# A three-block model on one core: x laid out twice, the first unit taken up as it arrives, weights split sooner, six output blocks sharing the first half

## The chip, the cores and the metric

The kernel runs on one core of one Trainium2 chip (trn2). The metric is the device time in microseconds (us). The engines are PE (TensorE: matmuls, with weight loads on its own queue PEld), DVE (VectorE), ACT (ScalarE), POOL (GpSimd) and SP (SyncE), which only issues DMAs here. They meet only through semaphores.

## What is computed

x is 512 tokens by 1024 features. Three layers follow one another: a gated linear recurrence (RG-LRU) with its MLP, a sparse attention layer with its MLP, and a second block of gated linear attention with a gated MLP. The change touches the first mixer alone:

```python
def rms_norm(x, g):
    y = xf * lax.rsqrt(jnp.mean(xf * xf, axis=-1, keepdims=True) + EPS)
    return y * g

def rglru_mixer(h, w_in, conv_w, conv_b, w_a, b_a, w_x, b_x, lam, w_out):
    gate, xr = jnp.split(h @ w_in, 2, axis=-1)          # 1024 -> 2 x 1024
    gate = jax.nn.gelu(gate)
    xc = conv_b + sum(xpad[:, k:k + S] * conv_w[k] for k in range(4))
    r = sigmoid(xc blockwise @ w_a + b_a); i = sigmoid(xc blockwise @ w_x + b_x)   # 4 blocks of 256
    log_a = -8 * r * softplus(-lam)
    a = exp(log_a); u = sqrt(-expm1(2 * log_a)) * (i * xc)
    hs = scan of h_t = a_t * h_{t-1} + u_t
    return (hs * gate) @ w_out
```

(The reference cut to this; `x = x + mix` and `x = x + mlp(rms_norm(x))` follow.)

## The kernel before, in words

**Layout.** Activations lie with features on the partitions: X, Ahi and Alo are eight blocks of 128 features by 512 tokens. Each product of float32 values is made of three matmuls in a 32-bit format with a shorter mantissa: hi times hi, lo times hi, hi times lo (`three`, L797 to L800). So every operand is split: ACT rounds it to the high part, DVE subtracts to get the low part.

**Units.** Weights come in units of 1024 by 256 (1 MB), numbered in the order in which they are used: 0 to 3 are xr (the recurrent half of w_in), 4 and 5 the two gate matrices (ga), 6 to 9 gate (the other half of w_in), 10 to 13 ro (w_out), then the MLP. A unit goes through `stage[u % 2]`, and there are two buffers each of `whi` and `wlo`. `hi(u)` on ACT (L1283) waits for the load and for the last product of unit u-2; `lo(u)` on DVE (L1791) waits for `hi(u)`; SP's `load(u)` (L552) waits for `lo(u-2)`; PE's `take_unit` waits for `lo(u)`. Unit 12 (ro 2) has hi and lo buffers of its own, inside Ahi and Alo.

**Blocks and banks.** A unit gives two blocks of 128 outputs by 512 tokens. Each of them takes one of six PSUM banks in a fixed ring order; `begin` waits until the bank's owner six places earlier has been read out. A full block is 24 matmuls of 512 columns; a block of ga is 6.

**Order of the work.** Every engine's order is written out by hand. PE: transposes of the identity, transposes of x, xr 0 and 1 in two halves of 256 tokens (L868), xr 2, the root (four matmuls that spread 1/rms over the partitions, L856), xr 3 to 7, ga (16 short blocks), gate 0 to 7, then ro: blocks 0 to 3 run over features 0 to 3 first and over 4 to 7 after that (L898), and ro 4 to 7 follow. DVE after the root: for each of eight blocks m `shifted(m + 1)` (scaling xr out of its bank, which frees it), `xc_low(m - 1)` and three convolution steps (L1879), with `lo(3)`, `lo(4)`, `lo(5)` behind blocks 2, 4 and 6; then `driven`, `bound`, `scan`, `mix`, `y_low` with `lo(6)` to `lo(11)` among them. ACT in the same stretch: `first_tap`, `XCh`, `gates(n)` (which read ga's banks and free them), `decay`, square roots, gelu, `y_high`, and `hi(u)`.

**The start.** SP loads x by tokens in four parts of 512 KB; PE transposes it in 32 steps into banks, ACT and DVE copy it to X (`copy_x`). Unit 0 comes in two column halves. The small vectors come as rows through 16 DMAs and three transposes (v0, v1, v2; 15 of the DMAs are POOL's). ACT and DVE square x by tokens for the root while xr 2 runs.

```python
        turn_identity(13)
        turn_x(0)
        ...
        turn_identity(10)
        for j in range(1, 4):
            turn_x(j)
```

Of the kernel before, what the change touches and what calls it, by code (L numbers as in the profile page):

```python
# [83 lines left out]
def program(nc, I, out, scratch):  # L84
# [83 lines left out]
    small2 = [("mix2", as_rows(I["norm_mix_2"][0, :]), 8), ("ffn2", as_rows(I["norm_ffn_2"][0, :]), 8),
              ("fin2", as_rows(I["norm_final_2"]), 8), ("gln", as_rows(I["gla_norm_2"][0, :]), 8),
              ("psc", as_rows(I["pool_scale_2"][0, :]), 8), ("bdf", as_rows(I["b_decay_fwd_2"][0, :]), 4),  # L170
              ("bdb", as_rows(I["b_decay_bwd_2"][0, :]), 4)]
    r1, r2, nr1, nr2 = {}, {}, 0, 0
    for name, ap, n in small1:
        r1[name] = nr1
        nr1 += n
    for name, ap, n in small2:
        r2[name] = nr2
        nr2 += n
    r1["mlp1"] = r1["mlp0"] + 8

    def c0(l, c):
        return cols0[:, 8 * l + c:8 * l + c + 1]

    def c1(name, i=0, n=1):
        return cols1[:, r1[name] + i:r1[name] + i + n]

    def c2(name, i=0, n=1):
        return cols2[:, r2[name] + i:r2[name] + i + n]
# [64 lines left out]
    s_load_a, s_hi_a, s_lo_a = sem("s_load_a"), sem("s_hi_a"), sem("s_lo_a")  # L253
    s_ahi_a, s_alo_a = sem("s_ahi_a"), sem("s_alo_a")
# [28 lines left out]
    ring.add(("x", 0, 0), ("x", 0, 1), "v0", *[("x", j, g) for j in range(1, 4) for g in range(2)], "v1", ("xr", 0), ("xr", 1), ("xr", 2),  # L283
             "root_x", ("xr", 3), "v2", *[("xr", m) for m in range(4, 8)])
# [92 lines left out]
    s_v0, s_v1, s_v2, s_xin = sem("s_v0"), sem("s_v1"), sem("s_v2"), [sem(f"s_xin{b}") for b in range(4)]  # L377
# [4 lines left out]
    FILL = {"rec": 0, "mlp0": 8, "att": 16, "mlp1": 24, "gla": 32, "ffn": 40}  # L382
# [163 lines left out]

    def whole(u):
        return max(k.stop for k, _, _ in units[u]), max(n.stop for _, n, _ in units[u])


    def sync_program(e):
# [28 lines left out]
    def gpsimd_program(e):  # L580
# [33 lines left out]
        for name, ap, n in small1:  # L614
            e.dma_start(rows1[r1[name]:r1[name] + n, :], ap).then_inc(s_v1, 16)
        for name, ap, n in small2:
            e.dma_start(rows2[r2[name]:r2[name] + n, :], ap).then_inc(s_v2, 16)
# [167 lines left out]
    def tensor_program(e):  # L785
# [47 lines left out]
        def turn_x(j):  # L833
            e.wait_ge(s_xin[j], 16)
            for g in range(2):
                transposes(("x", j, g), [xtok[:, j, (4 * g + c) * 128:(4 * g + c + 1) * 128] for c in range(4)])


# [4 lines left out]
        turn_identity(13)  # L843
        turn_x(0)
        e.wait_ge(s_v0, 16)
        ps = begin("v0")
        e.transpose(ps[:, 0:16], rows0[:, :], ident[0:16, 0:16]).then_inc(*ring.put("v0"))
        turn_identity(10)
        for j in range(1, 4):
            turn_x(j)  # L850
        ps = begin("v1")
        e.wait_ge(s_v1, 16 * len(small1))
        e.transpose(ps[:, 0:nr1], rows1[0:nr1, :], ident[0:nr1, 0:nr1]).then_inc(*ring.put("v1"))

# [8 lines left out]
        def other_columns():  # L863
            ps = begin("v2")
            e.wait_ge(s_v2, 16 * len(small2))
            e.transpose(ps[:, 0:nr2], rows2[0:nr2, :], ident[0:nr2, 0:nr2]).then_inc(*ring.put("v2"))

        def first_product(m, half):  # L868

            cols = slice(256 * half, 256 * half + 256)  # L870
            ps = ring.bank(("xr", m)) if half else begin(("xr", m))
            for k in range(8):
                if m == 0:
                    e.wait_ge(s_alo if half else s_alo_a, k + 1)
                i = three(ps[:, cols], whi[0][:, k, m * 128:(m + 1) * 128], wlo[0][:, k, m * 128:(m + 1) * 128], Ahi[:, k, cols], Alo[:, k, cols], k == 0, k == 7)
            if half:
                i.then_inc(*ring.put(("xr", m)))

        e.wait_ge(s_lo_a, 1)
        first_product(0, 0)  # L880
        take_unit(("xr", 0))
        first_product(1, 0)
        first_product(0, 1)
        first_product(1, 1)
        s = take_unit(("xr", 1))
        product(("xr", 2), s, 0, Ahi, Alo)
        first_root()
        product(("xr", 3), s, 128, Ahi, Alo)
        other_columns()
        gemm(("xr",), 4, Ahi, Alo, None, 0, first=4)  # L890
# [7 lines left out]
        for half in range(2):  # L898
            for m in range(4):
# [11 lines left out]
        gemm(("ro",), 4, YSh, YSl, None, 0, first=4)  # L911
# [368 lines left out]
    def scalar_program(e):  # L1280
        st = Steps(s_act)

        def hi(u):  # L1283
            s = u % 2
            nk, n = whole(u)
            e.wait_ge(s_w[s], t_load[u])
            if u >= 2:
                e.wait_ge(*ring.full(ends[u - 2]))
            e.activation(hi_of(u)[:, 0:nk, 0:n], stage[s][:, 0:nk, 0:n], ACT.Copy).then_inc(s_hi, 1)  # L1289
# [8 lines left out]
        def copy_x(j):  # L1298
            label = ("x", j, 0)
            e.wait_ge(*ring.full(label))  # L1300
            e.activation(X[:, 0:4, j * 128:(j + 1) * 128], ring.bank(label)[:, :].rearrange("p (c t) -> p c t", c=4), ACT.Copy).then_inc(*ring.take(label))
# [23 lines left out]
        for j in (0, 1):  # L1325
            if j:
                e.wait_ge(s_ssq, 1)
# [31 lines left out]
        for m in range(8):  # L1359
# [4 lines left out]
            if m == 7:  # L1364
                gates(0)
# [1137 lines left out]
```

## Time and profile before

| | us |
|---|---|
| median of 3 runs | 1870.34 (1869.83 to 1870.59) |
| the profiled execution's own time | 1869.64 |
| its span, first to last instruction | 1868.4 |
| PE busy | 1858.2 (99%) |
| DVE busy | 980.3 (52%) |
| ACT busy | 677.1 (36%) |
| POOL busy | 373.6 (20%) |

A busy share is the union of an engine's instructions. Matmuls overlap: a 512-column matmul is recorded with 390 ns, and the next one starts earlier than that, so the distance between two starts is what a matmul costs. Times in the rows below are from the span's start.

### The profile page before, as it was taken

What the parts mean: (1) busy time and instruction counts of PE and PEld (TensorE: products, weight loads), DVE (VectorE), ACT (ScalarE), POOL (GpSimd) and SP (SyncE); (2) the same over time, 40 slices, a digit from 0 to 9 for tenths busy, and PEclk for the clock granted to TensorE, in tenths of its full rate; (3) what the DMA queues carried; (4) which work ended last, traced back from release to release, by engine and by line L of the source; (5) the groups of instructions that cost most, each with busy time, mean ns of one, the idle gap of its engine ahead of it and who ended that gap; (6) DMA issues with size and microseconds to landing.
All of it is one profiled execution on the core that took longest, in us unless ns stands there. A gap on an engine that the chain in (4) does not pass through costs nothing.

```text
span 1868.4 us, 21946 instructions
## 1 busy us (share of the span) xinstructions
PE 1858.2 (99%) x8944; PEld 1509.4 (81%) x8944; DVE 980.3 (52%) x1328; ACT 677.1 (36%) x915; POOL 373.6 (20%) x333
## 2 busy tenths in 40 slices
PE   9999999999999999999999999999999999999998
PEld 8888888888877568888888879788887888888887
DVE  7885543334458864543434356666446554443433
ACT  6753322222234772321212335555323332222213
POOL 2004210010336783210101131111001311110102
PEclk9999999999999999999999999999999999999999
DMA  4322323322332103323223232222232322233231
GB/s 160 113 90 91 113 91 98 106 91 91 108 96 84 75 1 113 91 91 112 91 90 112 77 102 81 68 68 68 90 115 79 112 91 90 91 104 99 91 96 62
DMA packets 167171, 172.36 MB, mean 92 GB/s; under 512 B 7480, under 2 KB 164288, under 8 KB 167072
## 3 DMA queue, kind: packets, MB, share of 16 engines
q1 hardware_dynamic: 164576, 163.76, 27.3%
q0 software_dynamic: 2496, 7.21, 1.2%
q8 instruction: 71, 1.16, 0.3%
q14 instruction: 28, 0.23, 0.0%
HBM read 168.69 MB, written 2.14 MB: 91 GB/s over the span
## 4 chain that ended last, share of the span: by engine, by line
PE 98%; ACT 1%; DVE 0%; DMA 0%; issue 0%; POOL 0%; SPq 0%; ACTq 0%
PE bank L798 30%; PE bank L800 30%; PE bank L799 30%; PE bank L823 1%; PE bank L997 1%; PE bank L1021 1%; PE bank L1132 1%; PE bank L1150 1%; PE bank L999 1%; PE bank L945 0%; PE bank L1142 0%; PE bank L1116 0%; PE bank L1199 0%; PE bank L975 0%; DMA xtok<-in_x 0%; PE bank L981 0%
## 5 line engine op out<-in xcount | busy, mean ns | idle before, releaser
L798 PE MATMUL bank<-Ahi,whi 128*128 128x512 f32 (+2 forms) x1416 | 552.8, 390 | 0.9 <-DVE wlo L1836 0.5
L800 PE MATMUL bank<-Ahi,wlo 128*128 128x512 f32 (+2 forms) x1416 | 547.8, 387 | 0.0
L799 PE MATMUL bank<-Alo,whi 128*128 128x512 f32 (+2 forms) x1416 | 547.8, 387 | 0.0
L1797 DVE TENSOR_TENSOR wlo<-stage,whi 128x2048 fp32r<-128x2048 f32 (+2 forms) x146 | 333.2, 2282 | 379.5 <-ACT whi L1289 379.4
L1289 ACT ACTIVATE whi<-stage 128x2048 fp32r<-128x2048 f32 (+2 forms) x152 | 287.4, 1891 | 446.6 <-PE bank L800 446.6
L798 PEld LDWEIGHTS bank<-Ahi,whi 128*128 128x128 f32 (+1 forms) x1416 | 265.3, 187 | 63.3 <-issue 7.7
L800 PEld LDWEIGHTS bank<-Ahi,wlo 128*128 128x128 f32 (+1 forms) x1416 | 265.3, 187 | 55.1
L799 PEld LDWEIGHTS bank<-Alo,whi 128*128 128x128 f32 (+1 forms) x1416 | 265.4, 187 | 54.8 <-issue 1.2
L798 PE MATMUL bank<-Hhi,whi 128*128 128x512 f32 (+1 forms) x700 | 270.0, 386 | 0.0
L800 PE MATMUL bank<-Hhi,wlo 128*128 128x512 f32 (+1 forms) x700 | 269.8, 385 | 0.0
L799 PE MATMUL bank<-Hlo,whi 128*128 128x512 f32 (+1 forms) x700 | 269.8, 385 | 0.0
L642 POOL TENSOR_TENSOR hq<-ht 128x512 f32<-128x512 f32 x64 | 66.7, 1042 | 454.0 <-DVE ht L2010 454.0
L799 PEld LDWEIGHTS bank<-Hlo,whi 128*128 128x128 f32 x700 | 131.5, 188 | 26.5
L798 PEld LDWEIGHTS bank<-Hhi,whi 128*128 128x128 f32 x700 | 131.5, 188 | 26.3
L800 PEld LDWEIGHTS bank<-Hhi,wlo 128*128 128x128 f32 x700 | 131.5, 188 | 26.3
L1805 DVE TENSOR_TENSOR X<-X,bank 128x512 f32<-128x512 f32 x110 | 75.2, 683 | 80.0 <-PE bank L800 79.7
L1435 ACT ACTIVATE Hhi<-ht 128x512 fp32r<-128x512 f32 x64 | 40.6, 634 | 174.3 <-DVE ht L2010 174.3
L2013 DVE TENSOR_TENSOR Hlo<-hq,Hhi 128x512 fp32r<-128x512 f32 x64 | 44.3, 692 | 73.9 <-POOL hq L642 73.9
L779 POOL TENSOR_TENSOR fu<-fu,fg 128x512 f32<-128x512 f32 x22 | 28.4, 1293 | 253.9 <-DVE fu L2418 253.9
L721 POOL TENSOR_SCALAR pt<-pt,stat 128x128 f32<-128x128 f32 (+3 forms) x60 | 63.4, 1068 | 17.3 <-DVE stat L2103 16.7
L1292 ACT ACTIVATE Ahi<-X,cols 128x512 fp32r<-128x512 f32 x32 | 23.2, 726 | 92.1 <-DVE X L1805 89.8
L592 POOL TENSOR_TENSOR sqa<-X 128x512 f32<-128x512 f32 x5 | 5.2, 1042 | 244.6 <-DVE X L1805 244.6
(350 smaller groups left out, 2152.4 us busy)
## 6 DMA issues: line engine op xcount, KB each, us to landing
stage<-in_mlp_w_up SPq DMA_DIRECT2D x32, 1024.0 KB, 5.4
stage<-in_mlp_w_down SPq DMA_DIRECT2D x32, 1024.0 KB, 5.0
stage<-in_w_in SPq DMA_DIRECT2D x22, 1024.0 KB, 4.9
stage<-in_w_ffn_in SPq DMA_DIRECT2D x22, 1024.0 KB, 4.9
stage<-in_w_ffn_out SPq DMA_DIRECT2D x8, 1024.0 KB, 5.1
stage<-in_rec_w_in SPq DMA_DIRECT2D x7, 1024.0 KB, 5.2
stage<-in_att_w_in SPq DMA_DIRECT2D x6, 1024.0 KB, 5.4
stage<-in_rec_w_out SPq DMA_DIRECT2D x4, 1024.0 KB, 4.8
```

The source lines that it names most:

```text
L642: e.tensor_tensor(hq[n % 4][:, :], ht[n % 4][:, :], ht[n % 4][:, :], ALU.mult).then_inc(s_q, 1)
L721: e.tensor_scalar(p, p, stat[:, i % 8, 2:3], None, ALU.mult).then_inc(s_p, 1)
L779: e.tensor_tensor(fu[n % 4][:, :], fu[n % 4][:, :], fg[n % 4][:, :], ALU.mult).then_inc(s_fu, 1)
L798: e.matmul(ps, hi, rh, start=first, stop=False)
L799: e.matmul(ps, hi, rl, start=False, stop=False)
L800: return e.matmul(ps, lo, rh, start=False, stop=last)
L1289: e.activation(hi_of(u)[:, 0:nk, 0:n], stage[s][:, 0:nk, 0:n], ACT.Copy).then_inc(s_hi, 1)
L1292: e.activation(Ahi[:, m, :], X[:, m, :], ACT.Identity, scale=gc).then_inc(s_ahi, 1)
L1435: e.activation(Hhi[g % 2][:, m, :], ht[n % 4][:, :], ACT.Square).then_inc(s_hhi, 1)
L1797: e.tensor_tensor(lo_of(u)[:, 0:nk, 0:n], stage[s][:, 0:nk, 0:n], f32(hi_of(u)[:, 0:nk, 0:n]), ALU.subtract).then_inc(s_lo[s], 1)
L1805: e.tensor_tensor(X[:, m, :], X[:, m, :], ring.bank(label)[:, :], ALU.add).then_inc(*ring.take(label))
L2013: e.tensor_tensor(Hlo[g % 2][:, m, :], hq[n % 4][:, :], f32(Hhi[g % 2][:, m, :]), ALU.subtract).then_inc(s_hlo, 1)
```

## The change

x comes twice: `xT`, features by tokens, straight into X, and as before by tokens, for the squares alone. Both layouts and one array `cols` (128 by 153) with all the small vectors in columns are made outside the kernel. Unit 0 comes in four parts of two k-rows each (k counts blocks of 128 input features), unit 1 in two column halves. xr 0 and 1 run together, full width, k by k. The root moves into the middle of xr 3. Units 3 to 6 are split after conv blocks 1, 3, 5 and 7; gates of block pair 0 are read in ACT's steps 5 and 6. Units 7, 8 and 12 are split earlier too; six ro blocks share the first half.

```diff
 SP
+        load_x(0, 0, 1)                     # 256 KB
+        e.dma_start(cols[:, :], I["cols"]).then_inc(s_cols, 16)
+        load_first(0, s_load_a[0])          # k 0, 1 of unit 0: 256 KB
+        load_x(1, 1, 1)
+        load_x(2, 2, 2)                     # 512 KB
+        load_first(1, s_load_a[1])
+        load_first(2, s_load_a[2])
+        load_x(3, 4, 2)
+        load_x(4, 6, 2)
+        load_first(3, s_w[0])
+        (unit 1: columns 0:128, then 128:256)
+        for b in range(4):
+            e.dma_start(xtok[:, b, :], xtin[:, b, :]).then_inc(s_xtok[b], 16)
+        for u in range(2, len(units)):
             load(u)
 POOL
-        for name, ap, n in small1:
-            e.dma_start(rows1[r1[name]:r1[name] + n, :], ap).then_inc(s_v1, 16)
-        for name, ap, n in small2:
-            e.dma_start(rows2[r2[name]:r2[name] + n, :], ap).then_inc(s_v2, 16)
 PE
-        turn_identity(13) ... turn_identity(10), turn_x(0..3), v0, v1
+        turn_identity(24)
+        first = [begin(("xr", m)) for m in range(2)]
+        for k in range(8):
+            if k < 6:
+                e.wait_ge(s_lo_a, k // 2 + 1)
+            else:
+                take_unit(("xr", 0))
+            e.wait_ge(s_alo, k + 1)
+            for m in range(2):
+                i = three(first[m][:, :], ... k ...)
+        e.wait_ge(s_lo_b, 1)
+        product(("xr", 2), u_of["xr", 1], 0, Ahi, Alo)
+        (xr 3, with first_root() ahead of k == 4)
+        e.wait_ge(s_lo_c, 1)
+        product(("xr", 4), u_of["xr", 2], 0, Ahi, Alo)
+        product(("xr", 5), take_unit(("xr", 2)), 128, Ahi, Alo)
+        gemm(("xr",), 2, Ahi, Alo, None, 0, first=6)
         for half in range(2):
-            for m in range(4):
+            for m in range(6):
 ACT, hi(u)
-            if u >= 2:
+            if u == u_of["ro", 2]:
+                e.wait_ge(*ring.full(("gate", 7)))
+            elif u >= 2:
                 e.wait_ge(*ring.full(ends[u - 2]))
 ACT, the start (DVE likewise with the low parts)
+        first_hi(0), weights 0, first_hi(1), (2), weights 1, first_hi(3), weights 2,
+        first_hi(4), (5), (6), weights 3, first_hi(7), unit 1 in halves, squares of tokens 2, 3,
+        the square root, unit 2 in halves
 ACT, conv blocks m = 0..7
-            if m in (2, 4, 6):
-                hi(m // 2 + 2)
-            if m == 7:
-                gates(0)
+            if m % 2 == 1:
+                hi(m // 2 + 3)
+            if m in (5, 6):
+                gate_half(0, m - 5)
 ACT, after them
         gates(1)
-        hi(6)
         decay(0)
         decay(1)
         gates(2)
+        hi(7)
         decay(2)
         gates(3)
-        hi(7)
-        for c in range(3, 8):
+        for c in range(3, 6):
             decay(c)
         hi(8)
+        decay(6)
+        decay(7)
 ...
+        hi(12)                              # after gelu(7), ahead of y_high(6)
 DVE, the start
+        (lo of x and unit 0 part by part, unit 1 in halves, squares of tokens 0, 1, diag,
+         unit 2's first half, wait for the root, rstd, unit 2's second half)
 DVE, conv blocks
-            if m in (2, 4, 6):
-                lo(m // 2 + 2)
+            if m % 2 == 1:
+                lo(m // 2 + 3)
         e.wait_ge(s_xc, 8)
         xc_low(7)
 DVE, after them
         driven(0, 1, 2, 3)
-        lo(6)
         bound(0, 1)
         driven(4, 5)
+        lo(7)
         bound(2)
         driven(6, 7)
-        lo(7)
         bound(3)
         gate_out(0)
-        bound(4, 5, 6)
+        bound(4)
+        lo(8)
+        bound(5, 6)
         gate_out(1)
         bound(7)
-        lo(8)
 ...
         gate_out(7)
+        lo(12)
         mix(7)
         y_low(6)
         y_low(7)
```

The lines in brackets stand for code that says just that.

## Rows read from the trace of the kernel before

**Rows 1.** The page: busy time of the engines, and the chain that ended last.
```profile
PE 1858.2 (99%) x8944; PEld 1509.4 (81%) x8944; DVE 980.3 (52%) x1328; ACT 677.1 (36%) x915; POOL 373.6 (20%) x333
...
PE 98%; ACT 1%; DVE 0%; DMA 0%; issue 0%; POOL 0%; SPq 0%; ACTq 0%
```
**Rows 2.** Waits of PE: who for whom, us in total, times, longest.
```profile
PE bank L841 <- POOL ident L609: 1.8, 1, 1.8
...
PE bank L798 <- DVE wlo L1836: 0.5, 1, 0.5
```
**Rows 3.** Windows: stretch, length, busy us of PE, PEld, DVE, ACT, POOL; PEclk, DMA, GB/s.
```profile
1.75:7.25 5.50, 5.50 (x25) 5.05 (x26) 0.72 (x2) 1.86 (x4) 5.49 (x12) 1.00 0.97 306
7.35:8.05 0.70, 0.70 (x8) 0.66 (x7) 0.42 (x1) 0.24 (x1) 0.70 (x2) 1.00 1.04 405
...
58.09:79.84 21.75, 21.75 (x97) 18.02 (x96) 18.70 (x24) 19.75 (x26) 0.00 (x0) 1.00 0.39 125
...
96.80:128.00 31.20, 31.20 (x139) 25.82 (x139) 30.88 (x37) 17.33 (x24) 0.00 (x0) 1.00 0.30 102
```
**Rows 4.** Timeline of the start, all engines: start us, us, engine, line, operation.
```profile
0.81 0.37 SPq L562 DMA_DIRECT2D xtok<-in_x  x1
1.75 3.04 PE L841 MATMUL bank<-ident 128*128 128x128 f32 x13 [1.75 <-POOL ident L609]
4.58 1.92 PE L823 MATMUL bank<-ident,xtok 128*128 128x128 f32 x8
6.54 1.06 ACT L1315 ACTIVATE whi<-stage 128x1024 fp32r<-128x1024 f32 x1 [0.26 <-DMA stage<-in_rec_w_in]
...
11.79 0.36 PE L798 MATMUL bank<-Ahi,whi 128*128 128x256 f32 x1
15.36 0.38 PE L798 MATMUL bank<-Ahi,whi 128*128 128x256 f32 x1 [0.45 <-DVE wlo L1836]
```
**Rows 5.** Timeline of PE, 23.9 to 37: end of the halves, root, v2.
```profile
24.09 0.40 PE L798 MATMUL bank<-Ahi,whi 128*128 128x512 f32 x1
...
29.56 1.05 PE L860 MATMUL bank<-diag,ones 128*128 128x128 f32 x8
30.37 0.48 PE L798 MATMUL bank<-Ahi,whi 128*128 128x512 f32 x1
...
36.19 0.50 PE L798 MATMUL bank<-Ahi,whi 128*128 128x512 f32 x1
```
**Rows 6.** Timeline of DVE, 30 to 129.
```profile
31.43 1.29 DVE L1809 TENSOR_TENSOR pads<-bank,rstd 128x512 f32<-128x512 f32 x2
...
35.33 0.68 DVE L1809 TENSOR_TENSOR pads<-bank,rstd 128x512 f32<-128x512 f32 x1
...
38.95 0.68 DVE L1809 TENSOR_TENSOR pads<-bank,rstd 128x512 f32<-128x512 f32 x1
...
43.14 2.29 DVE L1797 TENSOR_TENSOR wlo<-stage,whi 128x2048 fp32r<-128x2048 f32 x1
...
68.57 1.29 DVE L1911 SCALAR_TENSOR_TENSOR XC<-tmp,XC 128x512 f32<-128x512 f32 x2
...
96.82 0.68 DVE L1925 TENSOR_TENSOR U<-U,XC 128x512 f32<-128x512 f32 x1
...
117.88 2.28 DVE L1797 TENSOR_TENSOR wlo<-stage,whi 128x2048 fp32r<-128x2048 f32 x1
...
125.71 2.29 DVE L1797 TENSOR_TENSOR wlo<-stage,whi 128x2048 fp32r<-128x2048 f32 x1
```
**Rows 7.** Timeline of ACT: gates(1) and gates(2).
```profile
67.76 1.25 ACT L1352 ACTIVATE TR<-bank,half 128x512 f32<-128x512 f32 x2
...
75.46 1.25 ACT L1352 ACTIVATE TR<-bank,half 128x512 f32<-128x512 f32 x2
```
**Rows 8.** Timeline of PE: the sixth block of ga, and the first matmul of ro 2.
```profile
64.89 0.39 PE L798 MATMUL bank<-XCh,whi 128*128 128x512 f32 x1
...
128.81 0.39 PE L798 MATMUL bank<-YSh,whi 128*128 128x512 f32 x1
```

More of the change, by code:

```diff
@@ L861, in first_root @@
             t.then_inc(*ring.put("root_x"))
[L863 to L890, printed above, removed]
+        first = [begin(("xr", m)) for m in range(2)]
[6 more added lines that the diff above has]
+            for m in range(2):
+                i = three(first[m][:, :], whi[0][:, k, m * 128:(m + 1) * 128], wlo[0][:, k, m * 128:(m + 1) * 128], Ahi[:, k, :], Alo[:, k, :], k == 0, k == 7)
+                if k == 7:
+                    i.then_inc(*ring.put(("xr", m)))
+        e.wait_ge(s_lo_b, 1)
+        product(("xr", 2), u_of["xr", 1], 0, Ahi, Alo)
+        s, ps = take_unit(("xr", 1)), begin(("xr", 3))
+        for k in range(8):
+            if k == 4:
+                first_root()
+            i = three(ps[:, :], whi[1][:, k, 128:256], wlo[1][:, k, 128:256], Ahi[:, k, :], Alo[:, k, :], k == 0, k == 7)
+        i.then_inc(*ring.put(("xr", 3)))
+        e.wait_ge(s_lo_c, 1)
+        product(("xr", 4), u_of["xr", 2], 0, Ahi, Alo)
+        product(("xr", 5), take_unit(("xr", 2)), 128, Ahi, Alo)
+        gemm(("xr",), 2, Ahi, Alo, None, 0, first=6)
         for n in range(4):
@@ L1296, in std_of, with first_hi @@
             e.activation(std[:, :], ring.bank(label)[:, :], ACT.Sqrt, bias=epsc[:, 0:1], scale=1.0 / n).then_inc(*ring.take(label))
[L1298 to L1301, printed above, removed]
-        def first_hi(half):
-            cols = slice(256 * half, 256 * half + 256)
-            for g in range(2):
-                for j in (2 * half, 2 * half + 1):
-                    e.wait_ge(*ring.free(("x", j, g)))
-                for c in range(4 * g, 4 * g + 4):
-                    e.activation(Ahi[:, c, cols], X[:, c, cols], ACT.Identity, scale=c0(0, c)).then_inc(s_ahi if half else s_ahi_a, 1)
+        def first_hi(k):
+            e.wait_ge(*x_there(k))
+            scaled_hi(k, c0(0, k))
@@ L1332, in scalar_program @@
         e.activation(ssq[:, 4:8], ssq[:, 0:4], ACT.Sqrt, bias=epsc[:, 0:1], scale=1.0 / 1024).then_inc(s_ssq, 1)
-        hi(2)
+        e.wait_ge(s_w[0], t_load[2])
+        e.wait_ge(*ring.full(ends[0]))
+        e.activation(whi[0][:, :, 0:128], stage[0][:, :, 0:128], ACT.Copy).then_inc(s_hi_c, 1)
+        e.activation(whi[0][:, :, 128:256], stage[0][:, :, 128:256], ACT.Copy).then_inc(s_hi, 1)
         def first_tap(m):
@@ L1409, in scalar_program @@
         hi(11)
-        for step, c in ((gelu, 7), (y_high, 6), (y_high, 7)):
-            step(c)
+        gelu(7)
+        hi(12)
+        y_high(6)
+        y_high(7)
         for what, m in product_order(8):
-            if what == "w" and m:
+            if what == "w" and m > 1:
                 hi(u_of["ro", m] + 1)
@@ L1814, in root @@
             e.wait_ge(s_rstd, RSTD[fill])
-        def copy_x(j):
-            label = ("x", j, 1)
-            e.wait_ge(*ring.full(label))
-            e.tensor_copy(X[:, 4:8, j * 128:(j + 1) * 128], ring.bank(label)[:, :].rearrange("p (c t) -> p c t", c=4)).then_inc(*ring.take(label))
-        def first_lo(half):
-            cols = slice(256 * half, 256 * half + 256)
-            for c in range(8):
-                e.wait_ge(s_ahi if half else s_ahi_a, c + 1)
-                e.scalar_tensor_tensor(Alo[:, c, cols], X[:, c, cols], c0(0, c), f32(Ahi[:, c, cols]), ALU.mult, ALU.subtract).then_inc(s_alo if half else s_alo_a, 1)
@@ L1882, in vector_program @@
             if m == 3:
-                e.wait_ge(*ring.full("v2"))
-                e.tensor_copy(cols2[:, 0:nr2], ring.bank("v2")[:, 0:nr2]).then_inc(*ring.take("v2"))
-                e.wait_ge(*ring.free("v2"))
                 e.tensor_scalar(gnh[:, :], c2("gln", 0, 8), 0.5, None, ALU.mult).then_inc(s_vec, 1)
```

218 lines of the change are left out of this document (105 added, 113 removed).

## The prediction

> **What bounds the kernel now.** The page first: PE is busy 99% of the span, and the chain that ended last is 98% PE [rows 1]. So nothing counts but what PE does and when it waits. The waits of PE come next: the longest is the 1.8 us before the first instruction, and the start has one more of note, 0.5 us [rows 2]. The timeline of the start shows where time can be had: PE's first product is issued at 11.79 [rows 4]. xr 0 and 1 in halves end at 24.09 [rows 5], and no row of PE's waits lies between there and 178.
>
> The last thing to read is who could hold PE up if it came sooner. DVE is busy 30.88 of the 31.20 us between 96.8 and 128.0, ACT 19.75 of 21.75 while PE does ga [rows 3]. That is the point of this case: PE never waits there, but it arrives only a little after its inputs. I take the sum against the profiled execution (1869.64; its span 1868.4); the median of the runs, 1870.34, is 0.70 above it, and that is added at the end.
>
> **The start.** Ahead of the first product now stand x block 0 (262 KB), `cols` (78 KB) and a quarter of unit 0 (262 KB), 0.60 MB on a queue whose first issue is at 0.81. Before, 0.53 MB were in use by 4.58 and 1.06 MB by 6.54 [rows 4], so 0.60 MB are there at about 4.8. ACT rounds the weight part in 0.63 (the length of a 128x512 gate step, two in 1.25 [rows 7]) and DVE subtracts in 0.69 (two in 1.29 [rows 6]): 6.2. The x part, earlier on the queue, is ready then too. But PE has 24 identity transposes ahead of it, and 13 took from 1.75 to 4.58, 0.218 each [rows 4]: they end at 7.0. So PE starts at 7.0, some 0.3 us before the distance between transposes halves (25 in 5.50 us up to 7.25, but 8 in 0.70 after 7.35 [rows 3]: the clock went from 1.2 to 2.4 GHz). That costs 0.15. I put the start at 7.1.
>
> A full-width matmul costs 21.75 / 96 = 0.2266 (16 blocks of 6 in ga [rows 3]), the first unit 48 of them, 10.9: it ends at 18.0. The feed keeps up: two k-rows cost PE 2.72, ACT and DVE some 2.0 (three at 0.63 or 0.69), and the queue 0.79 MB at 355 GB/s, the mean of 306 and 405 [rows 3], 2.2. Only k 2 is tight, at most 0.3 late. **So PE stands at 18.0 where it stood at 24.09: 6.1 sooner.** The three vector transposes, the 32 of x, their copies and POOL's 15 DMAs are in this; of them only v2, between xr 3 and 4, was outside, some 0.3 [rows 5]. At the start of xr 4 PE is 18.0 + 10.9 + 0.8 (root, 29.56 to 30.37 [rows 5]) = 29.7, against 36.19: 6.5 sooner.
>
> The new loads in between cost nothing as long as this holds: at 355 GB/s from 1.9, unit 1's halves land at 12.5 and 14 and are split by 16 and 17.5, ahead of 18.0 and 23.4; x by tokens (6.4 MB by then) lands at 20, its squares, square root and diag are ready at 23, against 26.2 when the root wants them; unit 2 (7.4 MB) lands at about 23, its first half is split at 25.5 against 29.7. If the queue were 3 us late here, PE would begin to wait, one for one.
>
> **The conv stage.** DVE's chain begins with the root, and the root is not 6 but 3.3 us sooner: 18.0 + 8.2 + 1.1 = 27.3 for its end, against 30.6. Behind it DVE copies rstd (0.7) and now also splits unit 2's second half (1.2), which before was done ahead of the root. `shifted(0)` starts at 29.2 instead of 31.43 [rows 6]: 2.2 sooner. A conv block takes 3.6 (35.33 to 38.95, two in the first 3.9), a split 2.2 net (43.14, 2.29) [rows 6]. The splits stand one block earlier, so unit 3 is ready at 39.0 (PE wants it at 40.6) and unit 4 at 49.2 (51.4): no wait. But `shifted(7)`, behind unit 5's split, ends at 59.1, and the sixth block of ga, which takes that bank, was issued at 64.89 [rows 8] and would now be at 58.3. **Wait 1: 0.8 to 0.9.**
>
> A fourth split, unit 6, now stands ahead of `xc_low(7)`. So `driven(0)` comes at 68.4, where it came at 68.57 [rows 6]: DVE's lead of 2.2 is spent on the moved split. ACT reaches `gates(1)` at 66.3 instead of 67.76 [rows 7], and `gates(2)` at 73.4 instead of 75.46, as a pair of gates and unit 6 lie earlier. Each frees banks for ga: block 10 finds its bank at 66.9 and PE came for it at 66.0 (**wait 2: 1.0**), block 12 waits 0.2, and block 14 wants the first bank of `gates(2)`, free at 74.0, at 72.6 (**wait 3: 1.5**). PE enters gate 0 at 76.8, 3.1 sooner, not 6.7.
>
> **The scan stage.** ACT now has unit 7 ahead of `decay(2)`: that rounding waits for ga's last block, 77.0, so ACT idles 1.3. Unit 8's rounding, ahead of `decay(6)`, waits for gate 1, and DVE waits behind it (`lo(8)` ahead of `bound(5)`), then `decay(7)` for `bound(5)`. Added up, `decay(7)` ends at about 95.1 and the first `scan` starts at 97.0; it was 96.82 [rows 6]. From there DVE's list is the same to `lo(11)` and has no gap: `lo(10)` done at 120.3 (117.88 + 2.28 before), `lo(11)` at 128.2 (before: 125.71 + 2.29 = 128.0 [rows 6]).
>
> PE comes to ro 0 at 120.4, just behind `lo(10)`, 3.0 sooner. ro 2 wants unit 11 at 125.9, having been served at 128.81, 0.8 after its split [rows 6, 8]: **wait 4: 2.4.** With six blocks sharing the first half, ro 4 comes at 133.7 and wants unit 12. Its rounding stands behind gelu(7), which waits for `gate_out(7)` behind `lo(11)`, its split 2.3 behind that: 135.0. **Wait 5: 1.2.** After it PE has 144 matmuls of ro, 32.6, and ends them at 167.7; before, from 128.81 with 168 matmuls left, 166.9 to 167.1. The second half wants y_low(7) at 142, and it is there at 137: the sharing hides that, but there was no wait to hide before.
>
> **The sum.** 6.5 sooner at xr 4, then 0.9 + 1.0 + 0.2 + 1.5 + 2.4 + 1.2 = 7.2 of waits: 0.7 later. From the MLP on the kernels are the same. 1869.6 + 0.7 = 1870.3 for the profiled execution, 0.70 more for the median: **1871.0**. A start that is earlier or later moves root, conv and all behind it alike, one for one.
>
> **A rule that speaks against the start.** The rows show the clock rising while PE did nothing but transposes [rows 3, 4]. The Trainium skill's page "TensorE: Matmul & The Clock Gate", section "Part 4: PE-mode transpose", says that transposes don't count as activity for the clock. By that rule the first products would meet the low clock. The trace disagrees: 8 transposes in 0.70 us before any product.
>
> **The rivals.** What can be told from no change is about 0.2%, 3.7 us.
>
> (a) PE keeps its lead: the splits come sooner by more than I reckon, and no wait opens. Then 1870.3 - 6.5 = 1863.8. For it: every split was moved forward. Against: DVE's 0.32 us of idle time in 31.2 [rows 3]; its list from the first scan on did not get shorter. Chance 0.06. Half of it: the waits of ga come, those of ro don't (DVE 3 us earlier at the first scan): 1867.4, chance 0.08, a third of it beyond 0.2%.
>
> (b) Slower: the clock falls in wait 4. It would be the longest in the first mixer, whose longest was 0.5 [rows 2]. Its price by the start, where PE worked from 1.75 to 7.25 at half speed [rows 3]: 5.5 / 2 = 2.8, and again after wait 5 if that too is enough: 1873.8 to 1876.6. It decides if a wait of 2.4 is enough to bring the clock down. Chance 0.05. The low clock at the start, by the page's rule, would cost the same 2.8 in one place; the rows say no, 0.01.
>
> (c) The first unit starves: loads of 256 KB land later than interpolated (every term of that queue is from transfers of 512 KB). 2 us late gives 1873.0, 4 us 1875.0. Chance 0.04 beyond 2 us.
>
> (d) The change doesn't do what it says: the start isn't earlier because PE still meets something at 11 us. Nothing in the order of the queue says so, 0.01, with the waits above at about 1875.
>
> **How the numbers follow.** The forecast case has 0.75 and its own range, 1868.5 to 1873.2: DVE's and ACT's lists 1% off over 100 us move lo(12) by 1, the start is known to 0.7. The range takes in the half of (a) and one fall of the clock: 1867.2 to 1874.0. Faster by over 0.2% (under 1866.6): 0.06 + 0.03 = 0.09. Slower by over 0.2% (over 1874.1): 0.07. Within: 0.84.
>
> **What the changed profile would show.** PE's first product at 7.0, xr 2 at 18.0, the root's copy at 27.4, `driven(0)` at 68 to 69, first scan at 97, and rows of PE's waits that weren't there: on DVE (pads, then wlo and ro_lo of ro 2 and ro 4) and on ACT (TR, tmp). If the first scan is at 94, or PE's waits between 50 and 140 sum to under 4, the sum is wrong; if the granted clock drops at 126 to 135, (b) is right.

## The result, and the profile after

The changed kernel takes **1872.41 us** (median of 22 runs, 1871.95 to 1873.09), the one before 1870.20 on the same chip (22 runs, 1869.57 to 1871.00): a ratio of 1.0012, 95% interval 1.0006 to 1.0017. That is 2.2 us slower, within the 0.2% that was called no change; forecast were 1871.0 and a range of 1867.2 to 1874.0. The profiled execution took 1872.89 (span 1871.7) against 1869.64 before: 3.25 more, where the sum had 0.7 more.

The waits of PE after (who for whom, us in total, times, longest), to be held against [rows 2]:
```profile
PE bank L795 <- DVE wlo L1783: 2.1, 1, 2.1
PE bank L795 <- ACT TR L1331: 1.9, 2, 1.2
PE bank L832 <- POOL ident L610: 1.7, 1, 1.7
...
PE bank L795 <- DVE wlo L1809: 0.6, 1, 0.6
```
The start's wait of 0.5 has gone, and one of 0.6 for the first weights (L1809) stands in its place. Two kinds weren't in [rows 2]: ACT's tanhs (the ga stage), and the low part of unit 11 (the 2.1). The timeline of the start, all engines (beside [rows 4]):
```profile
1.75 5.38 PE L832 MATMUL bank<-ident 128*128 128x128 f32 x24 [1.75 <-POOL ident L610]
...
3.88 0.72 ACT L1270 ACTIVATE Ahi<-X,cols 128x512 fp32r<-128x512 f32 x1 [1.58 <-DMA cols<-in_cols]
...
6.34 0.63 ACT L1282 ACTIVATE whi<-stage 128x512 fp32r<-128x512 f32 x1 [1.74 <-DMA stage<-in_rec_w_in]
...
7.01 0.69 DVE L1809 TENSOR_TENSOR wlo<-stage,whi 128x512 fp32r<-128x512 f32 x1 [1.52 <-ACT whi L1282]
...
7.75 0.50 PE L795 MATMUL bank<-Ahi,whi 128*128 128x512 f32 x1 [0.62 <-DVE wlo L1809]
7.86 0.73 ACT L1270 ACTIVATE Ahi<-X,cols 128x512 fp32r<-128x512 f32 x1 [0.89 <-DMA X<-in_xT]
```
PE's first product is at 7.75, not 7.0: not the transposes held it, which end at 7.13, but the first weights, which landed at 6.3. Windows of the changed kernel (columns as in [rows 3]):
```profile
4.00:6.30 2.30, 2.30 (x13) 2.30 (x12) 0.75 (x1) 0.60 (x1) 0.00 (x0) 1.00 0.74 144
53.12:78.16 25.04, 22.99 (x98) 17.72 (x96) 21.99 (x28) 19.25 (x25) 0.00 (x0) 1.00 0.36 112
96.80:128.00 31.20, 30.97 (x135) 24.77 (x133) 30.55 (x38) 19.62 (x26) 0.00 (x0) 1.00 0.23 79
129.00:134.00 5.00, 4.02 (x11) 3.17 (x12) 2.73 (x4) 2.24 (x2) 0.00 (x0) 0.66 0.62 201
122.14:169.82 47.68, 45.59 (x193) 37.24 (x193) 29.00 (x30) 15.20 (x16) 14.30 (x11) 0.96 0.32 100
```
The last row is the whole of the output product. Before, the same 192 matmuls had no gap:
```profile
123.36:166.88 43.52, 43.52 (x193) 36.04 (x192) 27.05 (x27) 14.73 (x15) 16.50 (x13) 1.00 0.33 106
```
So 47.68 - 43.52 = 4.16 us are lost there, and 25.04 - 21.75 = 3.29 in ga. And the clock fell: a mean granted clock of 0.66 over 5.00 us is 3.4 us at 1.2 GHz instead of 2.4, right behind the wait for unit 11. Where PE stands in each kernel, from the timelines of PE (us; each row is one profiled execution, the last column the median of the runs; the root of x lies 8.2 us of matmuls behind the end of unit 0, but 5.4 in before and in the last four rows). The profiled execution isn't always near the median: those of e2 (1866.97), e8 (1864.25) and e11 (1864.63) are the fastest of their runs, those of e4 (1872.92) and e5 (1869.41) the slowest, and that of e6 (1867.90) lies 1.4 above its median.

| kernel | PE's first product | root of x | ga 0 | gate 0 | ro 0 | up 0 | ro 0 to up 0 | median |
|---|---|---|---|---|---|---|---|---|
| before | 11.79 | 29.56 | 58.09 | 79.84 | 123.36 | 166.88 | 43.52 | 1870.20 |
| changed | 7.75 | 27.74 | 53.12 | 78.16 | 122.14 | 169.82 | 47.68 | 1872.41 |
| e1 splits late | 7.07 | 27.31 | 52.70 | 77.71 | 121.23 | 166.11 | 44.88 | 1868.95 |
| e2 start only | 7.44 | 26.87 | 54.79 | 77.05 | 120.56 | 164.29 | 43.73 | 1868.06 |
| e3 four blocks | 7.21 | 26.74 | 52.12 | 77.14 | 121.12 | 168.82 | 47.70 | 1872.04 |
| e4 busy wait | 7.55 | 27.77 | 53.15 | 78.17 | 122.15 | 169.37 | 47.22 | 1872.43 |
| e5 start and six | 7.11 | 27.91 | 57.40 | 79.16 | 122.68 | 166.65 | 43.97 | 1868.90 |
| e7 weights first | 6.92 | 27.97 | 57.51 | 79.27 | 122.79 | 166.31 | 43.52 | 1868.33 |
| e8 two taps | 7.07 | 27.28 | 52.80 | 74.56 | 118.08 | 161.60 | 43.52 | 1864.53 |
| e6 root early | 7.28 | 25.46 | 55.64 | 77.94 | 121.46 | 165.19 | 43.73 | 1866.52 |
| e9 root first | 7.63 | 24.52 | 53.55 | 75.84 | 119.36 | 163.12 | 43.76 | 1865.86 |
| e10 tokens sooner | 6.62 | 24.73 | 53.69 | 75.98 | 119.50 | 163.26 | 43.76 | 1865.94 |
| e11 best | 6.79 | 23.97 | 52.95 | 74.79 | 118.34 | 161.86 | 43.52 | 1865.48 |

From `up 0` to the end every one takes what the kernel before takes, within 0.8 us. The line "changed" tells the story: 5.0 us ahead at ga 0, 1.7 at gate 0, 1.2 at ro 0, 2.9 behind at up 0.

### The profile page after: what moved, and what is told of

Its sections match the earlier page's. It is cut to its first block, busy times and chain, and to the rows that moved or that the text cites. A ratio compares the mean times of both kernels' runs of the same rounds, so it can differ in the third digit from the quotient of the medians.

```text
span 1871.7 us, 21749 instructions
## 1 busy us (share of the span) xinstructions
PE 1856.7 (99%) x8858; PEld 1504.1 (80%) x8862; DVE 978.0 (52%) x1317; ACT 674.0 (36%) x907; POOL 365.0 (20%) x318
## 4 chain that ended last, share of the span: by engine, by line
PE 93%; DVE 3%; ACT 1%; issue 1%; DMA 0%; POOL 0%; another core or an unknown queue 0%; SPq 0%; DVEq 0%; ACTq 0%
PE bank L795 28%; PE bank L796 28%; PE bank L797 28%; PE bank L820 1%; PE bank L973 1%; PE bank L997 1%; DVE XC L1882 1%; DVE wlo L1783 1%; PE bank L1108 1%; PE bank L1126 1%; PE bank L975 1%; PE bank L921 0%; PE bank L1118 0%; PE bank L1092 0%; PE bank L951 0%
## 5 line engine op out<-in xcount | busy, mean ns | idle before, releaser
L795 PE MATMUL bank<-Ahi,whi 128*128 128x512 f32 (+1 forms) x1400 | 550.4, 393 | 1.3 <-DVE wlo L1809 0.6
L796 PE MATMUL bank<-Alo,whi 128*128 128x512 f32 (+1 forms) x1400 | 545.3, 389 | 0.0
L797 PE MATMUL bank<-Ahi,wlo 128*128 128x512 f32 (+1 forms) x1400 | 545.2, 389 | 0.0
L1783 DVE TENSOR_TENSOR wlo<-stage,whi 128x2048 fp32r<-128x2048 f32 (+2 forms) x144 | 329.1, 2285 | 381.5 <-ACT whi L1267 381.4
L1267 ACT ACTIVATE whi<-stage 128x2048 fp32r<-128x2048 f32 (+2 forms) x150 | 283.4, 1889 | 450.9 <-PE bank L797 450.9
L1270 ACT ACTIVATE Ahi<-X,cols 128x512 fp32r<-128x512 f32 x40 | 28.8, 723 | 96.0 <-DVE X L1791 92.5
```

Source lines behind the costliest of these rows:

```text
L795: e.matmul(ps, hi, rh, start=first, stop=False)
L796: e.matmul(ps, hi, rl, start=False, stop=False)
L797: return e.matmul(ps, lo, rh, start=False, stop=last)
L1270: e.activation(Ahi[:, m, :], X[:, m, :], ACT.Identity, scale=gc).then_inc(s_ahi, 1)
L1783: e.tensor_tensor(lo_of(u)[:, 0:nk, 0:n], stage[s][:, 0:nk, 0:n], f32(hi_of(u)[:, 0:nk, 0:n]), ALU.subtract).then_inc(s_lo[s], 1)
```

## The experiments

Each of the three sets ran beside the kernel before on one chip: its medians there are 1870.58 (e1 to e4), 1870.46 (e5 to e8) and 1870.39 (e9 to e11). Ratios are to these. The changed kernel itself wasn't run beside them; where a text says how much less a variant takes than the changed kernel, 1872.41 is from another chip, on which the kernel before read 1870.20, 0.2 to 0.4 lower.

**e1: the splits of units 7 and 8 back in their old places.** On ACT:
```diff
         gates(2)
-        hi(7)
         decay(2)
         gates(3)
-        for c in range(3, 6):
+        hi(7)
+        for c in range(3, 8):
             decay(c)
         hi(8)
-        decay(6)
-        decay(7)
```
and on DVE `lo(7)` behind `driven(6, 7)`, `lo(8)` behind `bound(7)`.

> The changed kernel with one part undone: the splits of units 7 and 8 go back to where they stood before (hi of 7 behind gates(3), hi of 8 behind the last decay, lo of 7 behind driven(7), lo of 8 behind bound(7)). Theory A (the order of the splits gave the lead back): the two splits ahead of the decays hold ACT and DVE up by about 2.5 us between 75 and 92 us, nothing of PE needs them so soon; the first scan then ends near 96 us instead of 98.7, the 2.1 us wait ahead of output block 2 is gone, and the kernel takes 2.5 to 3.2 us less than the changed one, about 1869.5 us. Rival B (the late start of PE and its stalls in the first unit are all of it): the scans come no sooner, the time stays at 1872.4. Rival C (units 7 and 8 had to be split sooner): PE waits for lo of unit 7 or 8 at the gates' blocks and the time rises by 1 us or more.

1868.95 us (1868.40 to 1869.63), ratio 0.9992 (0.9983 to 1.0001): 3.5 us less than the changed kernel. The timeline of DVE of the changed kernel, where the splits stand ahead of the decays' bounds:
```profile
80.36 2.29 DVE L1783 TENSOR_TENSOR wlo<-stage,whi 128x2048 fp32r<-128x2048 f32 x1 [2.58 <-ACT whi L1267]
...
91.32 2.29 DVE L1783 TENSOR_TENSOR wlo<-stage,whi 128x2048 fp32r<-128x2048 f32 x1 [2.00 <-ACT whi L1267]
...
98.73 0.69 DVE L1908 TENSOR_TENSOR U<-U,XC 128x512 f32<-128x512 f32 x1 [0.30 <-ACT U L1383]
```
and of e1, the end of unit 8's split and the first scan:
```profile
93.28 2.29 DVE L1781 TENSOR_TENSOR wlo<-stage,whi 128x2048 fp32r<-128x2048 f32 x1
95.49 0.69 DVE L1906 TENSOR_TENSOR U<-U,XC 128x512 f32<-128x512 f32 x1
```
DVE stood 2.58 and 2.00 us behind the two roundings on ACT. These take 1.92 each and had waited for PE themselves, 1.45 (unit 7) and 0.26 (unit 8), and further on ACT stood 2.26 for DVE, ahead of its last decay. Without that the first scan comes 3.2 us sooner, 0.4 of it from a better start. PE's 2.1 us wait for unit 11 is gone, and with it the fall of the clock. Rivals B and C are out: the scans do come sooner, ga takes 25.01 us as before the edit (25.04), and no gate block waits. What is left of the loss in the output product is 44.88 - 43.52 = 1.36, and a row that had been hidden names most of it (PE stood ahead of block 4, where 1.1 is lost over two matmuls):
```profile
PE bank L795 <- DVE ro_lo L1781: 0.8, 1, 0.8
```

**e2: the changed start alone.** e1 with, besides, units 3 to 6 and the first gates where they stood before, `range(4)` in the output's first half and unit 12 split in the old place.

> The changed start (x by features, first unit as it arrives, squares from tokens), everything behind it in the order of before: units 3 to 8 split in the old places, gates(0) behind the last tap, four blocks share the output's first half, unit 12 split in the old place. Theory A: the start's lead over before at the end of unit 0 is 4.5 us; 2.8 us of it go to a wait for lo of unit 3 near 45 us, the rest arrives: 1.5 us faster than before, about 1868.7 us, 3.7 us faster than the changed kernel. Rival B (the start itself brings nothing, because the loads of units 2 and 3 come later than before): the same as before or slower, 1870.2 or more. Rival D (the new order is needed to carry the start): slower than the changed kernel's 1872.4.

1868.06 us (1866.97 to 1869.70), ratio 0.9987 (0.9979 to 0.9996): faster than before by 2.5 us, 4.3 less than the changed kernel. Its waits of PE up to 182 us:
```profile
PE bank L795 <- DVE wlo L1781: 2.2, 1, 2.2
PE bank L832 <- POOL ident L610: 1.8, 1, 1.8
PE bank L795 <- DVE wlo L1807: 1.1, 1, 1.1
```
The wait for unit 3, at 43.7, is the only row behind the start (2.2 us, expected 2.8). ga takes 22.26 instead of 25.04 and the output product 43.73, 0.5 and 0.2 above the kernel before. This profile is of the fastest of its runs. So the start is worth something, and what was laid over it, order and sharing together, took more than that.

**e3: four blocks share instead of six**, `range(4)` and `first=4` in the changed kernel, unit 12 still early.

> The changed kernel with one part undone: four blocks instead of six share the output's first half; unit 12 is still split early. Theory A (six blocks hide nothing here, since the wait they were to cover is moved to the halves' units 11 and 12): the work that PE does ahead of the second half shrinks by 3.2 us, a wait of 1.0 to 1.2 us for the last YSl blocks takes the place of the one for lo of unit 12, and the time is the changed kernel's within 0.3 us. Rival D (six blocks carry the change): PE waits 2.5 to 3 us at YSl 4 to 7, and the kernel is 1.5 to 3 us slower. Rival E (sharing six costs by itself): faster by 1 us.

1872.04 us (1871.21 to 1873.77), ratio 1.0008 (1.0000 to 1.0017). From ro 0 to up 0:
```profile
121.12:168.82 47.70, 45.63 (x193) 37.23 (x194) 29.07 (x31) 15.45 (x16) 16.15 (x13) 0.96 0.35 111
```
47.70 against 47.68: to share six instead of four hides nothing here. Both have the same wait for unit 11 and the same fall of the clock. The wait of 1.0 to 1.2 for the last YSl blocks that was expected isn't there; PE comes to them late, behind the slow matmuls. The difference of the medians, 0.4, is within what the start does from run to run.

**e4: wait 4 filled**, `turn_identity(18)` ahead of output block 2.

> The changed kernel with 18 identity transposes, written into a bank that nothing reads, ahead of output block 2: about 2 us of work at full clock, laid into the wait of 2.1 us for lo of unit 11. It tells what the fall of the granted clock after that wait costs. Theory A: the clock stays at full speed between 130.4 and 133.8 us; the 1.6 us of slow matmuls are saved, of which about 1 us comes back as the wait for lo of unit 12 that they had covered: 0.4 to 0.7 us faster than the changed kernel, 1871.9. Rival F (the clock's fall is the whole of the loss against the forecast): 1.6 us faster. Rival G (the transposes don't count for the clock, or delay block 2): no change, or up to 1 us slower.

1872.43 us (1871.72 to 1872.92), ratio 1.0010 (1.0001 to 1.0019): no change as a whole, so the number expected was missed. In the stage:
```profile
122.15:169.37 47.22, 46.27 (x211) 38.01 (x211) 29.02 (x30) 15.19 (x16) 14.30 (x11) 1.00 0.32 102
129.00:134.00 5.00, 4.88 (x25) 3.93 (x24) 2.74 (x4) 2.23 (x2) 0.00 (x0) 1.00 0.60 203
```
The clock stays up, a wait of 0.8 for ro_lo comes back at block 4, and the stage is 0.46 shorter, at the lower end of what theory A had. Behind the root of the MLP this execution lost 0.48 again, most of it in two small steps near 630 and 1417 us, far from the edit; why stays open. So the fall of the clock costs about half a microsecond here, since the wait for unit 12 lay under the slow matmuls. The changed kernel's own runs say the same: a fall of 3.4 us takes 0.0009 off a run's mean clock, so the four with a mean of 1.000 had none, and they average 1872.16; the thirteen with 0.998 average 1872.61.

**e5: e2 with six blocks and the early unit 12 put back.**

> The start-only kernel (1868.06 us) with one part of the change put back: unit 12 is split early, behind unit 11 and ahead of the last two YS blocks, and six blocks share the output's first half. Theory A (the pair costs by itself: the split of unit 12 takes 2.0 us of ACT and 2.3 us of DVE ahead of mix(7) and y_low(6, 7), and PE must have unit 12 before it may go on to block 4's first half): a wait of about 1.2 us ahead of output block 4, and 1.2 us more than the start-only kernel, about 1869.2. Rival D (six blocks give PE 3.2 us of work to lay under the wait for the last YSl blocks): the same time or faster, 1868.1 or less.

1868.90 us (1868.03 to 1869.41), ratio 0.9991 (0.9982 to 1.0000): 0.84 more than e2 by the medians, whose runs spread over 2.7 us. Its profile doesn't show the wait of 1.2: block 4 waited 0.3, since PE came to ro 0 2.1 us later than in e2 (1.0 from the start, 1.1 from a fall of the clock behind the wait for unit 3, near 45 us), and
```profile
131.49 2.29 DVE L1782 TENSOR_TENSOR ro_lo<-stage,ro_hi 128x2048 fp32r<-128x2048 f32 x1 [2.50 <-ACT ro_hi L1267]
```
had ended at 133.8. Had the clock not fallen, PE would have come 1.1 sooner and stood there some 1.4, an estimate that no run shows. That the pair gains nothing is shown by e3 and e5; what it costs alone, between 0.2 (43.97 against 43.73 here) and 1.4 us (e1), isn't settled.

**e6: the root of x ahead of block 3**, and the low part of unit 2's second half behind `shifted(1)`, in e2.

> The start-only kernel with the root of x a half block sooner: its matmuls ahead of block 3 instead of in its middle, and the low part of unit 2's second half behind shifted(1). DVE begins its chain of shifted, taps and XCl at the copy of the root, and from there on PE follows DVE up to the gates. Theory A: shifted(0) begins about 1.0 us sooner, the wait for lo of unit 3 shrinks by as much or more, PE waits up to 0.6 us for the diagonal ahead of the root, and the whole takes 0.8 to 1.0 us less: 1867.1 us. Rival H (in the start-only kernel the wait for lo of unit 3 is set by its load, not by DVE's chain): the wait stays, no change.

1866.52 us (1866.06 to 1868.86), ratio 0.9981 (0.9972 to 0.9990): by the medians 1.5 less than e2, more than was expected. So rival H is out: it isn't the load that holds unit 3 but DVE's chain from the root, and in e2 DVE has no idle time of note from 31.3 until it has split unit 3. The profile doesn't show the gain, since it is of a slow run of e6 and a fast one of e2: unit 0 ended 1.3 later than in e2, the root's copy stood until 28.41 behind a split that had waited for unit 2's load, and gate 0 comes at 77.94 against 77.05.

**e7: the first weights ahead of x's first block and the columns**, in e2.

> The start-only kernel with the first quarter of unit 0's weights loaded ahead of x's first block and the columns, and split as it comes. In the five profiles of this start the queue moved between 144 and 295 GB/s from 4.0 to 6.3 us and the first weights landed between 5.64 and 6.32 us, though they stand third. Theory A (the first unit is bound by the sum of the bytes, 3.1 MB, and by the slow stretch, whichever transfer is in it): PE starts 0.2 to 0.6 us sooner but stalls as much longer in the unit; first unit's end and the time as the start-only kernel's within 0.3 us, 1868.1. Rival I (the landing of the first weights sets the unit's end): 0.5 us or more faster.

1868.33 us (1867.31 to 1870.69), ratio 0.9990 (0.9982 to 0.9999). PE began at 6.92, 0.5 sooner than in e2, and then stood at its third k-row:
```profile
11.52 0.50 PE L795 MATMUL bank<-Ahi,whi 128*128 128x512 f32 x1 [1.60 <-DVE wlo L1807]
```
The root is at 27.97, 1.1 later than in e2. Rival I is out: weights that land first don't end the unit sooner. That the sum of the bytes sets its end, as theory A has it, fits but isn't shown; its end of 19.8 lies 1.2 later than the earliest of the profiles before it, with the same bytes. Here too the clock fell behind the wait for unit 3; windows of e7 and of e2 over that place:
```profile
45.00:50.50 5.50, 5.50 (x18) 4.33 (x19) 5.30 (x11) 2.92 (x4) 0.00 (x0) 0.69 0.61 191
```
```profile
44.00:49.50 5.50, 5.50 (x25) 4.50 (x25) 5.29 (x11) 3.02 (x4) 0.00 (x0) 1.00 0.61 194
```

**e8: two taps of the convolution on DVE instead of three**, in e2 (`range(1, 3)`). The last tap is left out, so the output isn't that of the model; the run prices DVE's work.

> The start-only kernel with the convolution's last tap left out (its output differs from the reference's there): DVE does two multiply-adds for each block instead of three, 8 x 0.83 us = 6.6 us of DVE's work less between 30 and 68 us, and nothing less on ACT or PE. Theory A (DVE's chain from the root's copy to the last XCl holds PE there; behind it ACT and PE take over at once): 2.5 to 3 us faster, 1865.2 us, and PE's wait for lo of unit 3 falls from 2.2 us to about 0.5 us. Rival J (DVE is the bound all through): 6 us faster. Rival K (ACT's taps, copies and tanhs are the bound, or the loads of units 2 and 3): less than 0.5 us.

1864.53 us (5 runs, 1864.25 to 1864.86), ratio 0.9968 (0.9955 to 0.9980): 3.5 less than e2, of 6.6 us taken away, and 0.5 to 1.0 more than theory A had. No row of PE's waits is left between 20 and 120 us, and from the root to gate 0 PE takes 47.28 instead of 50.18. DVE's chain is the bound there, and once it is some 3 us shorter PE is.

**e9: the copy of the root ahead of unit 2's split**, in e6. On DVE:
```diff
-        e.wait_ge(s_hi_c, 1)
-        e.tensor_tensor(wlo[0][:, :, 0:128], stage[0][:, :, 0:128], f32(whi[0][:, :, 0:128]), ALU.subtract).then_inc(s_lo_c, 1)
         e.wait_ge(*ring.full("root_x"))
...
         shifted(0)
+        e.wait_ge(s_hi_c, 1)
+        e.tensor_tensor(wlo[0][:, :, 0:128], stage[0][:, :, 0:128], f32(whi[0][:, :, 0:128]), ALU.subtract).then_inc(s_lo_c, 1)
```

> The root-early kernel (1866.52 us) with what stands around the root's copy put in another order: on DVE the copy of the root and shifted(0) go ahead of the low part of unit 2's first half (that split waited until 27.27 us for a load, and the copy stood behind it until 28.41 although the root was there near 26.5), the low part of its second half goes behind shifted(2); on ACT the softplus of lambda with its two table loads (3.1 us) goes ahead of the wait for unit 2. Theory A (DVE's chain from the root's copy holds PE up to the gates): the copy begins near 26.6 us, DVE's idle time of 2.39 and 0.68 us there shrinks to about 1.6, and the kernel is 0.8 to 1.4 us faster than the root-early one, 1865.4. Rival L (ACT's first tap or the load of unit 2 sets it anyway): no change, 1866.5.

The low part of unit 2's second half goes one block later too, and on ACT the softplus stands ahead of unit 2; which of the three wins what isn't separated. 1865.86 us (1865.34 to 1867.82), ratio 0.9978 (0.9969 to 0.9987): 0.7 less than e6 by the medians, a little under what was expected, and the intervals of the two overlap. The copy stands 1.2 us behind the root's first matmul now; in e6 it was 3.0:
```profile
25.68 0.69 DVE L1842 COPY rstd<-bank 128x512 f32<-128x512 f32 x1 [1.31 <-PE bank L840]
```

**e10: x by tokens loaded ahead of unit 1's second half**, in e9.

> As the last, and x by tokens is loaded ahead of the second half of unit 1, whose split moves behind the squares and the diagonal; the first tap goes ahead of unit 2's split on ACT, the low part of unit 2's first half behind block 0's taps on DVE. Theory A: the squares are there 1.2 us sooner, the root is multiplied near 24.2 us instead of 25.5, shifted(0) and the first taps start 1 to 1.5 us sooner, and 0.5 to 1.2 us of it arrive: 1864.6 us. Rival M (unit 3's load is issued only once unit 1 is split, and comes too late then): PE's wait for lo of unit 3 grows by what was won and the time is that of the last kernel or worse.

1865.94 us (1865.22 to 1866.47), ratio 0.9977 (0.9968 to 0.9986): no change. The diagonal was there at 22.5, but PE comes to the root only at 24.73, when block 2 is done, and DVE is idle for 2.06 ahead of the copy. It isn't rival M, no wait for unit 3 is left; PE itself had become the bound of the root. The edit also brought a wait of its own, 0.5 at 31.7 for unit 2's first half, about as long as the one for unit 3 that it took away:
```profile
PE bank L795 <- DVE wlo L1885: 0.5, 1, 0.5
```

**e11: e10 with the steps of ACT and DVE from 60 to 135 us in another order** (decays and gates nearer to their banks, `hi(7)` behind `decay(4)`, each scan, mix and `y_low` as soon as its input is there).

> As the last, and the steps of ACT and DVE from 60 to 135 us reordered by hand: decays and gates(2), gates(3) closer to their banks, unit 7 split behind decay(4), scans, mixes and y_low each as soon as the other engine gives them. Theory A (between the gates and the output's first half DVE and ACT together set the end, and their idle time there is what an order can win): 0.4 to 0.8 us less, 1864.0 us. Rival N (from the gates on PE is the bound, the order behind them is hidden): no change; then the time from the first gate block to the first output block stays at 43.5 us and the second half follows without a wait in both.

1865.48 us (9 runs, 1864.63 to 1865.88), ratio 0.9974 (0.9965 to 0.9984): **4.9 less than before** and 6.9 less than the changed kernel, the fastest that computes the whole model. Against e10 it is 0.5 less by the medians, whose ranges overlap; the stages say where it comes from: ga takes 21.84 instead of 22.29 and the output 43.52 instead of 43.76, and from gate 0 to ro 0 PE was the bound in both (43.55 and 43.52), as rival N had it for that stretch. Its windows of gates, output and ga:
```profile
74.79:118.34 43.55, 43.55 (x194) 36.00 (x192) 42.31 (x52) 32.86 (x43) 0.00 (x0) 1.00 0.28 91
118.34:161.86 43.52, 43.52 (x194) 36.04 (x192) 28.15 (x28) 14.20 (x14) 16.16 (x13) 1.00 0.34 110
52.95:74.79 21.84, 21.84 (x97) 17.94 (x96) 17.81 (x23) 18.55 (x24) 0.00 (x0) 1.00 0.40 127
```
PE has no idle time in any of them: it is 5.1 ahead of before at ga 0 and still 5.0 at up 0, so what the start wins there arrives whole.

## Why the prediction held, and where it was off

**What held.** That PE would arrive sooner everywhere and wait where it had never waited: the sum had 7.2 us of waits, the profile shows 3.29 in ga, 0.46 more from gate 0 to ro 0 than before, mostly a wait for `lo(10)`, and 4.16 in the output with what the clock took: 7.9. The ga stage was given 3.6 of them: by the timeline PE lost 0.4, 0.9, 0.3 and 1.5 there at blocks 5, 10, 12 and 14, where the sum had 0.9, 1.0, 0.2 and 1.5. `driven(0)` was forecast at 68.4 and came at 69.48, the first scan at 97.0 and came at 98.73, 1.1 and 1.7 late behind a root that was 1.5 late. Wait 4 was forecast at 2.4 and is 2.2 (2.47 from one matmul to the next, less one of 0.23). The statement that the sharing hides a wait that wasn't there is e3's result.

**The term that was mis-sized: the first unit.** "So PE stands at 18.0 where it stood at 24.09". It ended at 19.6, 1.6 later (the root is at 27.74 where 18.0 + 8.2 was reckoned): 0.65 at PE's start, 7.75 instead of 7.1, and 0.9 in stalls for the next k-rows, 0.3 to 0.4 each ahead of k 1 and of k 2. The step that failed is that "the feed keeps up", with 355 GB/s for loads of 256 KB taken from loads of 512 KB. The queue moved 144 GB/s from 4.0 to 6.3 us, where before it moved 321 in the same stretch; only from 8 to 12 us did it move the 363 that was reckoned with. It isn't a fixed price: the same instructions in e3 and e2 moved, in the same stretch,
```profile
4.00:6.30 2.30, 2.30 (x13) 2.30 (x12) 0.75 (x1) 0.94 (x2) 0.00 (x0) 1.00 0.91 295
```
```profile
4.00:6.30 2.30, 2.30 (x15) 2.13 (x13) 0.75 (x1) 0.59 (x2) 0.00 (x0) 1.00 0.75 232
```
and the root lies between 26.74 and 27.91 in the seven profiles with this start and this place of the root: 0.5 to 1.7 late, never early. In the eleven profiles with this order of the queue the first weights landed between 4.9 and 6.3 (forecast: 4.8) and unit 0 ended between 18.5 and 20.0. The rate of that one stretch doesn't order them: e5 moved 266 GB/s there and ended unit 0 at 19.7, having stood 1.1 ahead of k 1. This was rival (c), at less than the 2 us that was given as its price. Why loads are slow there stays open. In e7, where the first quarter of the weights landed at 4.3, the long stall (1.6) was for the second quarter, so it isn't tied to that one transfer.

**The rivals.** (a) fell: e1 shows that the splits that were moved sooner made DVE's list later, by 2.8 us. (b) happened: the clock fell behind wait 4, which had been given 0.05 with a price of 2.8. That price was the wrong size: 3.4 us at the lower level are 1.7 us of work, the next wait lay under it, and e4 finds 0.46. (d) is out, PE's first product came 4.0 us sooner. The half of (a), in which ga's waits come and those of the output don't, is out by the 4.16 there.

**Why the numbers agreed.** 1.5 too little for the start, 0.5 for ro 0, 0.6 for the output (mostly the clock), 0.3 too much for ga: 2.3 up to the MLP and 0.3 more behind it in the profiled execution, of which the median shows 1.4. All but ga's are on one side, as nearly all the unknowns were; a range with more room above than below would have said so. That the total stayed inside the range is owed to the waits, which came where they were forecast, and in part to luck: the late start alone took half of the 3.0 that the range left above.

**What wasn't seen.** That the waits were a matter of the order: the sum took the moved splits as the cost of the start. What each part is worth can be read from the medians: 2.5 us won by the start (e2 against before), against 0.9 given to the early units 3 to 6 and to the pair of six blocks and unit 12 (e1 against e2), and 3.5 to units 7 and 8 (changed against e1, with the clock's 0.5 in it). 2.5 - 0.9 - 3.5 is 1.9 slower. That is no check of the parts, since the three steps lead from before to changed by themselves; it differs from the 2.2 that was measured only because the kernel before read 0.4 higher beside the experiments. The 3.5 is clear of the spread of the runs; the 0.9 isn't, with e2's runs 2.7 us apart. Unit 7's part and unit 8's weren't told apart.

## What to carry to other kernels

A rounding moved ahead of other work in a queue costs its own time only if its input is there, and more if it isn't: `hi(7)` and `hi(8)` waited 1.45 and 0.26 for the engine that was to be served, and a second engine stood 2.58 and 2.00 behind them. When a start is made faster, list for each wait that opens what stands ahead of the releaser in its queue that nobody needs yet, before paying for it with more shared work further down. And an engine that was never late in the old profile has a slack that must be written down as a number at each hand-over (here 0.8 us at unit 11): a gain larger than the slack buys only a wait.

## What the hardware did that was not expected

The clock fell after waits of 2.1 to 2.2 us, and not always: in e2 the wait for unit 3 (2.2 us) left it up, in e5 and e7 a wait of the same length was followed by a fall. The wait for unit 11 was followed by one in both profiles that have it empty (changed and e3), yet not in the four runs of the changed kernel with a mean clock of 1.000. Of e2's eleven runs the five with a mean clock of 0.999 of full speed lie between 1866.97 and 1868.06, the six at 0.998 or less between 1867.87 and 1869.70. One such fall costs the stage from the root to gate 0 1.1 us (51.25 in e5 and 51.30 in e7, against 50.18 in e2).

With 18 identity transposes in wait 4 the clock stayed at full speed (e4, one profile; none of its eleven runs has a mean under 0.999, of the changed kernel's 22 thirteen have). And the 24 at the start, ahead of any product, take less time where the clock comes up among them; the timelines of PE of the changed kernel and of e5:
```profile
1.75 5.38 PE L832 MATMUL bank<-ident 128*128 128x128 f32 x24 [1.75 <-POOL ident L610]
```
```profile
1.75 4.19 PE L832 MATMUL bank<-ident 128*128 128x128 f32 x24 [1.75 <-POOL ident L610]
```
That is read from the distances between matmuls: the PEclk column shows 1.00 for the start in every profile, also where 24 transposes take 5.38 us, 0.22 each, and doesn't tell the level there. In the changed kernel the clock came up behind the transposes, and the first products, 0.22 to 0.24 apart from the second on, already run at full speed.

The Trainium skill's page "TensorE: Matmul & The Clock Gate", section "Part 4: PE-mode transpose", says that transposes don't count as activity for the clock; these 128x128 ones of f32 did at the start, and the one profile of e4 agrees.
